# One of the two gate products of each attention tile moved between the turn of its probabilities and their products with the values

## The chip, the cores and the metric

The kernel runs on one core of a Trainium2 chip. The metric is the device time of one execution in microseconds (us). TensorE is called PE here, VectorE DVE, ScalarE ACT, GpSimd POOL and SyncE SP, as in the profile.

## The reference

Two blocks run one after the other over 256 tokens of width 1024, in fp32. The first has a convolution, a gated linear attention and a mixture of 64 experts. The second, in which the change lies, has a linear recurrence beside an attention over 64 selected keys, a feed-forward part and a last gate. Of the second block this matters:

```python
logits = logits + bias                                  # 8 heads, masked to the selected keys
probs = softmax(logits, axis=-1)
o = einsum('btngk,btknd->btngd', probs, v_sel)
yb = o @ w_attn_br
merged = sigmoid(gate_a) * ya + sigmoid(gate_b) * yb    # gate_b: 1024 columns of xn @ w_in
x = x + merged @ w_out
xn = rmsnorm(x, ffn_norm)
up = xn @ w_up
...
```

## The kernel before

Each engine has its program written out by hand, in one fixed order, and waits on named semaphores. The tokens form two tiles of 128 (t = 0 and 1).

**Tasks and banks.** Everything that PE computes is a task with a name, and a task takes one of the eight PSUM banks. The list `_tasks()` names all tasks in PE's order, and `_bank_table()` deals the banks out in turn: with eight banks, a task has the bank of the task eight places ahead of it in the list. `take_bank(task)` makes PE wait until that earlier task's bank was read out, `full(ins, task)` reports a result, and `wait_full` and `read` are the reader's side.

**The attention of the second block.** PE computes the logits, `log0_0` to `log0_3` for tile 0 and `log1_0` to `log1_3` for tile 1 (L1016), then two branch products `ya2`, `ya3`. DVE adds the bias to a bank of logits (L2085) and copies it out with the mask (L2088); that frees the bank. After the last one DVE takes the row maxima (L2091, L2093), ACT the exponentials (L1419), and DVE the inverse of the sums (L2097) and the scaling of the probabilities (L2099), which sets `probs_ready`. PE turns the probabilities by transposes, tasks `pt` (L1028), ACT copies them out (L1433), PE multiplies them with the values, tasks `pv` (L1035), and ACT copies these out (L1437). Tile 0 has 2 `pt` tasks, tile 1 has 4; each tile has 2 `pv` tasks. The gate products `gd0` to `gd3` (sigmoid of them is gate_b, L1092 on ACT) depend on none of this; PE does two of them behind each tile's `pv`.

ACT's order around it, which the change leaves alone, is this:

```python
for t in range(TT):
    ...                                   # 8 exponentials of tile t, L1419
    if t == 0: weights_high(1, "gd1")
    else: per_chunk(["gd0", "gd1"], ...)
    ...                                   # pt copies L1433, then pv copies L1437
    if t == 0: weights_high(1, "gd3")
```

**Weights in two parts.** A large weight is multiplied as a high and a low part. SP loads it into a ring (one unit of 2 MB), ACT rounds it to the high part in two halves (`weights_high`, L1107), and POOL subtracts to get the low part, in four pieces a half (`weights_low`, L533). A product task of this kind (L595) of 128x256 runs, for each of its two columns blocks, 16 matmuls with the high part and then 8 with the low part, 48 in all; the first wait for `high_ready`, the others for `low_ready`. Units are named after the last task that uses them: `gd1` serves gd0 and gd1, `gd3` serves gd2 and gd3, `yb1` and `yb3` the attention's output product (tasks `yb0` to `yb3`), `mo0_1` and `mo1_1` the merged output product (tasks `mo`). ACT makes the high part of `yb1` behind the rounding of both tiles' `pv` results (L1444, whose low part is L1584 on DVE), then that of `yb3`, `mo0_1` and `mo1_1`. POOL follows unit by unit; of `mo1_1` it does half and DVE the other half (L1584). After the `yb` tasks DVE gates them (L2117, L2120), ACT rounds (L1454), and PE goes on with `mo`, the turn L662, and the feed-forward products, all on L595.

The functions that the change touches follow.

Of the kernel before, what the change touches and what calls it, by code (L numbers as in the profile page):

```python
# [47 lines left out]
NH, NKV, HD = 8, 2, 128  # L48
# [26 lines left out]
def _tasks():  # L75
    names = []
    names += ["g0", "g1", "a0", "a1", "g2", "g3", "a2", "a3", "k0", "k1", "fl", "z0", "z1"]
    names += [f"v{u}_{t}" for u in range(2) for t in range(2)] + ["q0", "q1"]
    names += ["r0", "r1", "kdt0", "kdt1", "r2", "r3"] + [f"kv{i}" for i in range(8)] + ["ga0", "ga1"]
    names += [f"o{h}" for h in range(4)] + ["ga2", "ga3", "osum0", "osum1", "csum"]  # L80
    names += ["gb0", "gb1", "csq", "gb2", "gb3"]
    names += [f"yg{j}" for j in range(4)] + [f"yc{j}" for j in range(4)]
    names += [f"mix{u}_{t}" for t in range(2) for u in range(2)]
    names += ["x1t0", "x1t1", "lg0", "x1t2", "x1t3", "lg1", "pos"]
    first = list(names)
    n2 = [f"x2t{j}" for j in range(4)] + ["relb", "kiwi_k", "kiwi_w"]
    n2 += [f"lx{j}" for j in range(4)] + ["wi"] + [f"lg_{j}" for j in range(4)]
    n2 += ["kk", "vv", "qi0", "qi1"] + [f"dots{t}_{j}" for t in range(2) for j in range(4)]
    n2 += [f"lr{j}" for j in range(4)] + [f"li{j}" for j in range(4)]
    n2 += ["ksum"] + [f"qq{j}" for j in range(4)]  # L90
    n2 += ["gc0", "gc1"] + ["qsum"] + ["gc2", "gc3", "ya0", "ya1"]
    for t in range(2):
        n2 += [f"log{t}_{j}" for j in range(4)]
    n2 += ["ya2", "ya3"]
    for t in range(2):
        n2 += [f"pt{t}_{s}_{k}" for s in range(t + 1) for k in range(2)] + [f"pv{t}_{k}" for k in range(2)]
        n2 += [f"gd{2 * t}", f"gd{2 * t + 1}"]
    n2 += [f"yb{j}" for j in range(4)] + ["mo0_0", "mo1_0", "mo0_1", "x3t0", "x3t1", "mo1_1", "x3t2", "x3t3"]
    for i in range(6):
        n2 += [f"fg{i}_0", f"fg{i}_1", f"fu{i}_0", f"fu{i}_1"]  # L100
    n2 += [f"dn{u}_{t}" for u in range(2) for t in range(2)]
    for t in range(2):
        n2 += [f"x4t{2 * t}", f"x4t{2 * t + 1}"] + [f"pp{u}_{t}" for u in range(2)]
    n2 += [f"pg{u}_{t}" for t in range(2) for u in range(2)]
    return first, n2
# [41 lines left out]
def build(nc, a, out):  # L147
    with ExitStack() as ctx:
# [80 lines left out]
        v2 = slab[:, 7, 512:1024].rearrange("p (t n) -> p t n", t=TT)  # L229
# [12 lines left out]
        prob_t = slab[:, 5, :].rearrange("p (s h t) -> p s h t", s=TT, h=NH)  # L242
# [39 lines left out]
        def take_bank(task):  # L282

            b, use = BANK[task]
            if use:
                nc.tensor.wait_ge(S(f"bank_read{b}"), use)
            return bank(task)

        def full(ins, task):

            ins.then_inc(S(f"bank_full{BANK[task][0]}"), 1)
# [10 lines left out]
        def wait_read(eng, *tasks):  # L302

            for task in tasks:
                b, use = BANK[task]
                eng.wait_ge(S(f"bank_read{b}"), use + 1)
# [264 lines left out]
        def _(pe):  # L571
            mm = nc.tensor.matmul
            units = [0, 0]

            def unit(part=0, cols_=512):


                name = UNITS[part][units[part]]
                s = units[part] % STREAM
                units[part] += 1  # L580
                w = ring[:, s, :].rearrange("p (c n) -> p c n", n=cols_)
                if name not in SPLIT[part]:
                    wait_landed(pe, part, name)
                    return w
                high = ring[:, STREAM + SPLIT[part].index(name) % 2, :].rearrange("p (c n) -> p c n", n=cols_)
                return high, w, split_count(part, name)
# [29 lines left out]
                    ins = one(r32(low[:, c, wcol]), r32(x[0][:, c, xcol]), False, c == DC - 1)  # L616
                return ins

            def chan_major(w, x, tasks, arrive=None):

                for i, task in enumerate(tasks):
                    o = take_bank(task)
                    for m in range(2):
                        f = P * (2 * i + m)
                        last = products(o[:, T * m:T * m + T], w, x, False, slice(f, f + P), slice(0, T), i,
                                        arrive=None if i + m else arrive)
                    full(last, task)
# [40 lines left out]
            w = ring[:, 0, :].rearrange("p (c n) -> p c n", c=DC)  # L668
            chan_major(w, xT, ["g0"])
            w = unit()[:, :, 256:512]  # L670
# [10 lines left out]
            o = take_bank("fl")  # L681
            for c in range(DC):
                last = mm(o[0:RANK, 0:T], w_flr[:, c, :], xT[:, c, :], start=c == 0, stop=c == DC - 1)
# [3 lines left out]
            for j in range(2):  # L687
                o = take_bank(f"z{j}")
                for m in range(2):
                    f = P * (2 * j + m)  # L690
                    last = mm(o[:, T * m:T * m + T], slab[0:RANK, 10, f:f + P], slab[0:RANK, 10, 512:512 + T],
                              start=True, stop=True)
# [8 lines left out]
            for t in range(TT):  # L701
                o = take_bank(f"kdt{t}")
                for h in range(H1):
                    last = nc.tensor.transpose(o[:, P * h:P * h + P], half(5, 0)[:, h, P * t:P * t + P], ident[:])
# [4 lines left out]
            for n in range(NCH):  # L709
                b = CHUNK * (n % 2)  # L710
                for hp in range(2):
                    task = f"kv{2 * n + hp}"
                    o = take_bank(task)
                    for m in range(2):
                        h = 2 * hp + m
# [8 lines left out]
            for h in range(H1):  # L724
                o = take_bank(f"o{h}")
                for m in range(2):
                    for n in range(NCH):
                        st = states(n, h)[:, P * m:P * m + P]
                        last = mm(o[:, T * m + CHUNK * n:T * m + CHUNK * n + CHUNK], st,  # L729
                                  half(7, 0)[:, h, CHUNK * n:CHUNK * n + CHUNK], start=True, stop=True)  # L730
# [207 lines left out]
            xn = xn_parts  # L938
# [82 lines left out]
            for t in range(TT):  # L1021

                pe.wait_ge(S("probs_ready"), t + 1)
                for s in range(t + 1):
                    for k in range(2):
                        o = take_bank(f"pt{t}_{s}_{k}")
                        for m in range(4):
                            last = nc.tensor.transpose(o[:, P * m:P * m + P], lgt[:, 4 * k + m, P * s:P * s + P],  # L1028
                                                       ident[:])
                        full(last, f"pt{t}_{s}_{k}")  # L1030
                wait_read(pe, *[f"pt{t}_{s}_{k}" for s in range(t + 1) for k in range(2)])
                for k in range(2):
                    o = take_bank(f"pv{t}_{k}")
                    for s in range(t + 1):
                        last = mm(o[:, 0:512], v2[:, s, HD * k:HD * k + HD],  # L1035
                                  prob_t[:, s, 4 * k:4 * k + 4, :].rearrange("p h t -> p (h t)"),
                                  start=s == 0, stop=s == t)
                    full(last, f"pv{t}_{k}")
                chan_major(unit(1), xn, [f"gd{2 * t}", f"gd{2 * t + 1}"])
            pe.wait_ge(S("att_low"), 2)  # L1040
            chan_major(unit(1), att_parts, ["yb0", "yb1"])
            chan_major(unit(1), att_parts, ["yb2", "yb3"])
# [1254 lines left out]
```

## Time and profile before

| | |
|---|---|
| median of 3 runs | 1736.12 us (1735.61 to 1736.6) |
| time of the profiled execution | 1736.04 us |
| its span, first to last instruction | 1734.3 us |
| mean granted clock of PE | 0.89 |
| PE busy | 1363.6 us (79% of the span) |
| POOL busy | 609.2 us (35%) |
| ACT busy | 429.1 us (25%) |
| DVE busy | 423.0 us (24%) |

The time is 1.7 us above the span of the same execution. The shares are means over very different stages: the expert stage in the middle of the span waits for transfers, and the attention lies near 1,385 to 1,440 us, behind it. What the change is worth is read from that part and from what follows it. PE and PEld are the matmuls and the weight loads of the one TensorE; PEclk 1.00 is 2.4 GHz and 0.50 is 1.2 GHz.

### The profile page before, as it was taken

To read this page: it belongs to the slowest core of one execution; us is meant where nothing else is said; L and a number is where in the kernel's file an instruction comes from. 1 tells how busy PE (TensorE), PEld (TensorE's weight loads), DVE (VectorE), ACT (ScalarE), POOL (GpSimd) and SP (SyncE) were. 2 spreads that over 40 slices of the span, in tenths; PEclk is the share of its full clock that TensorE was granted. 3 is DMA by queue.
4 is the path that set the end of the run, shared out by engine and by line. 5 is a ranking of instruction groups with operands and counts; after the bars stand their busy time and mean duration, and the time that the engine had idled before them with its cause. 6 is when DMAs were issued, how large, how long until landed. Compare 5 with 4: busy or idle time off the path is not lost.

```text
span 1734.3 us, 21607 instructions
## 1 busy us (share of the span) xinstructions
PE 1363.6 (79%) x9196; PEld 983.1 (57%) x9196; DVE 423.0 (24%) x901; ACT 429.1 (25%) x542; POOL 609.2 (35%) x485
## 2 busy tenths in 40 slices
PE   7999998677557746675666576657799999899998
PEld 7899996333123313331333133222699988899986
DVE  3995554000000000000000000000416642233203
ACT  4444741000000000000000000000547563544434
POOL 6886790000000000000000000000587958688894
PEclk9999999888788878877888788778899999999999
DMA  9453477999999999999999999999445444455551
GB/s 366 147 192 108 176 270 293 384 428 428 427 429 428 428 429 428 429 429 429 429 428 428 429 428 429 429 428 419 164 167 209 156 161 146 146 195 187 176 192 54
DMA packets 46058, 539.56 MB, mean 311 GB/s; under 512 B 4440, under 2 KB 8544, under 8 KB 14624
## 3 DMA queue, kind: packets, MB, share of 16 engines
q1 hardware_dynamic: 42704, 532.44, 75.5%
q0 software_dynamic: 1184, 3.94, 0.6%
q10 hardware_dynamic: 2096, 2.11, 0.4%
q8 instruction: 56, 0.92, 0.2%
q14 instruction: 18, 0.15, 0.0%
HBM read 537.41 MB, written 1.06 MB: 310 GB/s over the span
## 4 chain that ended last, share of the span: by engine, by line
PE 64%; DMA 30%; DVE 2%; SPq 1%; ACT 1%; issue 1%; POOL 1%; DVEq 0%; ACTq 0%
PE bank L595 38%; DMA ring<-in_w 18%; PE bank L823 13%; DMA slab<-in_w 10%; PE bank L808 6%; PE bank L880 2%; DMA ring<-in_units 1%; SPq L408 1%; PE bank L869 1%; POOL ring_parts L533 1%; ACT ring_parts L1107 0%; PE bank L1035 0%; PE bank L989 0%; PE bank L729 0%; PE bank L835 0%
## 5 line engine op out<-in xcount | busy, mean ns | idle before, releaser
L533 POOL TENSOR_TENSOR ring_parts<-ring,ring_parts 128x512 fp32r<-128x512 f32 x448 | 594.6, 1366 | 1007.2 <-ACT ring_parts L1107 1007.1
L595 PE MATMUL bank<-slab_parts,ring_parts 128*128 128x256 f32 x3328 | 498.2, 285 | 2.1 <-DVE rows_parts L1968 2.1
L595 PEld LDWEIGHTS bank<-slab_parts,ring_parts 128*128 128x128 f32 x3328 | 458.1, 193 | 4.4 <-issue 3.1
L823 PE MATMUL bank<-ring,slab 128*32 128x512 f32 x1472 | 254.9, 674 | 168.6 <-DMA slab<-in_w 88.1
L823 PEld LDWEIGHTS bank<-ring,slab 128*32 128x32 f32 x1472 | 68.4, 122 | 340.8 <-issue 339.1
L1107 ACT ACTIVATE ring_parts<-ring 128x2048 fp32r<-128x2048 f32 x114 | 212.0, 1910 | 169.5 <-PE bank L595 167.2
L869 PE MATMUL bank<-ring,slab 128*32 128x512 f32 x752 | 139.2, 724 | 140.5 <-DMA slab<-in_w 70.5
L595 PE MATMUL bank<-rows_parts,ring_parts 128*128 128x256 f32 x752 | 187.2, 286 | 0.0
L869 PEld LDWEIGHTS bank<-ring,slab 128*32 128x32 f32 x752 | 37.4, 130 | 226.1 <-issue 225.4
L595 PE MATMUL bank<-ring_parts,slab_parts 128*128 128x512 f32 (+1 forms) x672 | 160.5, 388 | 3.9 <-POOL ring_parts L533 2.8
L1868 DVE TENSOR_TENSOR slab<-slab,bank 128x512 f32<-128x512 f32 x16 | 11.0, 687 | 578.7 <-PE bank L823 578.7
L595 PEld LDWEIGHTS bank<-rows_parts,ring_parts 128*128 128x128 f32 x752 | 146.5, 195 | 0.5 <-issue 0.5
L595 PEld LDWEIGHTS bank<-ring_parts,slab_parts 128*128 128x128 f32 x672 | 125.7, 190 | 31.7 <-POOL ring_parts L533 3.7
L823 PE MATMUL bank<-slab 128*32 128x512 f32 x512 | 130.5, 668 | 0.0
L808 PEld LDWEIGHTS bank<-slab 128*128 128x128 f32 x512 | 124.2, 334 | 7.4 <-issue 4.2
L808 PE MATMUL bank<-slab 128*128 128x128 f32 x512 | 122.9, 401 | 1.5 <-DVE slab L1851 1.5
L1546 DVE SCALAR_TENSOR_TENSOR bank<-slab,cols,bank 128x255 f32<-128x255 f32 (+28 forms) x232 | 88.0, 468 | 0.1
L1224 ACT ACTIVATE slab<-bank 128x512 f32<-128x512 f32 x16 | 9.6, 597 | 282.6 <-PE bank L823 276.6
L1232 ACT ACTIVATE slab<-bank 128x512 f32<-128x512 f32 x16 | 9.6, 597 | 282.0 <-PE bank L869 282.0
L1876 DVE COPY slab<-bank 128x512 f32<-128x512 f32 x16 | 11.1, 692 | 276.3 <-PE bank L869 276.3
L869 PE MATMUL bank<-slab 128*32 128x512 f32 x272 | 74.6, 709 | 4.0 <-DMA slab<-in_w 3.4
L1220 ACT ACTIVATE slab<-bank 128x512 f32<-128x512 f32 x16 | 9.6, 597 | 272.0 <-PE bank L823 260.2
(302 smaller groups left out, 941.5 us busy)
## 6 DMA issues: line engine op xcount, KB each, us to landing
ring<-in_w SPq DMA_DIRECT2D x143, 2048.0 KB, 19.8
ring<-in_units SPq DMA_DIRECT2D x59, 2048.0 KB, 8.4
slab<-in_w SPq DMA_DIRECT2D x49, 2048.0 KB, 25.3
ring<-in_units SPq DMA_DIRECT2D x2, 1024.0 KB, 9.2
slab<-bias_scratch ACTq DMA_DIRECT2D x2, 1024.0 KB, 8.6
slab<-in_xT SPq DMA_DIRECT2D x1, 1024.0 KB, 5.0
rows<-in_ln_g POOLq DMA_DIRECT2D x2, 512.0 KB, 17.9
slab<-in_x SPq DMA_DIRECT2D x1, 1024.0 KB, 5.3
```

Source lines behind the costliest of these rows:

```text
L408: sp.dma_start(dst, src).then_inc(S(f"expert_landed{step % 2}{j}" if place is None else "apart_landed"), 16)
L533: ins = g.tensor_tensor(r32(w_q), w_q, r32(high_q), ALU.subtract)
L595: return mm(out_, l, r, start=start and first, stop=stop and last)
L808: last = mm(b[:, P * (c % 4):P * (c % 4) + P], tok(0)[:, t, c::DC], sel[:, t, :, :].rearrange("p j s -> p (j s)"), start=t == 0, stop=t == 1)
L823: last = mm(b[CAP * j:CAP * j + CAP, :], xg[:, c, CAP * j:CAP * j + CAP], wt[j][:, c, :], start=c == 0, stop=c == DC - 1, tile_position=(0 ...
L869: last = mm(b[CAP * j:CAP * j + CAP, :], hid_t[:, m, CAP * j:CAP * j + CAP], wt[j][:, 512 * hf:512 * hf + 512], start=m == 0, stop=m == 3, ...
L880: last = mm(acc[t][hf][:], spread[:, P * t:P * t + P], y_sb[:, 512 * hf:512 * hf + 512], start=False, stop=ends, skip_group_check=again)
L1107: A(r32(high), w, ACT.Copy).then_inc(S("high_ready"), 1)
L1220: A(slab[:, 1, 0:512], low_bank[:], ACT.Copy).then_inc(S("xg0_copied"), 1)
L1546: ins = stt(out_, src[:, c, 0:T - lag], wc, sum_[:, lag:T], ALU.mult, ALU.add)
L1868: tt(hid, silu_sb, up_bank[:], ALU.mult).then_inc(S("hid_ready"), 1)
L1876: v.tensor_copy(y_sb[:, 512:1024], high_bank[:]).then_inc(S("y1_copied"), 1)
```

## The change

The task list, and with it the banks, and the order on PE. The second gate product of a tile stays where it was; the first goes ahead of the tile's `pv` tasks. Nothing is computed differently, and no instruction is added or dropped.

```diff
     for t in range(2):
-        n2 += [f"pt{t}_{s}_{k}" for s in range(t + 1) for k in range(2)] + [f"pv{t}_{k}" for k in range(2)]
-        n2 += [f"gd{2 * t}", f"gd{2 * t + 1}"]
+        n2 += [f"pt{t}_{s}_{k}" for s in range(t + 1) for k in range(2)]
+        n2 += [f"gd{2 * t}"] + [f"pv{t}_{k}" for k in range(2)] + [f"gd{2 * t + 1}"]
...
-            def chan_major(w, x, tasks, arrive=None):
+            def chan_major(w, x, tasks, arrive=None, between=None):
 
                 for i, task in enumerate(tasks):
+                    if i and between:
+                        between()
                     o = take_bank(task)
...
-                wait_read(pe, *[f"pt{t}_{s}_{k}" for s in range(t + 1) for k in range(2)])
-                for k in range(2):
-                    o = take_bank(f"pv{t}_{k}")
-                    for s in range(t + 1):
-                        last = mm(o[:, 0:512], v2[:, s, HD * k:HD * k + HD],
-                                  prob_t[:, s, 4 * k:4 * k + 4, :].rearrange("p h t -> p (h t)"),
-                                  start=s == 0, stop=s == t)
-                    full(last, f"pv{t}_{k}")
-                chan_major(unit(1), xn, [f"gd{2 * t}", f"gd{2 * t + 1}"])
+                def values(t=t):
+                    wait_read(pe, *[f"pt{t}_{s}_{k}" for s in range(t + 1) for k in range(2)])
+                    for k in range(2):
+                        o = take_bank(f"pv{t}_{k}")
+                        for s in range(t + 1):
+                            last = mm(o[:, 0:512], v2[:, s, HD * k:HD * k + HD],
+                                      prob_t[:, s, 4 * k:4 * k + 4, :].rearrange("p h t -> p (h t)"),
+                                      start=s == 0, stop=s == t)
+                        full(last, f"pv{t}_{k}")
+                chan_major(unit(1), xn, [f"gd{2 * t}", f"gd{2 * t + 1}"], between=values)
```

On PE, at tile 0, the order before is as follows: L1028 is `pt`, L1035 is `pv`, L595 here is `gd0`. `bank_readN` is the wait for bank N to be read out. The banks of the logits are visible in the list: `log1_0` has bank 4, `log1_1` bank 5, `log1_2` bank 0, `log1_3` bank 1.

```order
L1028 MATMUL bank2<-ident,slab 128x128 [waits bank_read2,probs_ready]
L1028 MATMUL bank2<-ident,slab 128x128 x3
L1028 MATMUL bank3<-ident,slab 128x128 [waits bank_read3]
L1028 MATMUL bank3<-ident,slab 128x128 x3
L1035 MATMUL bank4<-slab 128x512 [waits bank_read4,bank_read3,bank_read2]
L1035 MATMUL bank5<-slab 128x512 [waits bank_read5]
L595 MATMUL bank0<-slab_parts,ring_parts 128x256 [waits high_ready,bank_read0]
```

The same place now (L1030 is `pt`, L1038 is `pv`, L595 with bank 4 is `gd0` and with bank 1 is `gd1`; the other matmuls of `gd0`, alike, are left out):

```order
L1030 MATMUL bank2<-ident,slab 128x128 [waits bank_read2,probs_ready]
L1030 MATMUL bank2<-ident,slab 128x128 x3
L1030 MATMUL bank3<-ident,slab 128x128 [waits bank_read3]
L1030 MATMUL bank3<-ident,slab 128x128 x3
L595 MATMUL bank4<-slab_parts,ring_parts 128x256 [waits high_ready,bank_read4]
...
L1038 MATMUL bank5<-slab 128x512 [waits bank_read5,bank_read3,bank_read2]
L1038 MATMUL bank0<-slab 128x512 [waits bank_read0]
L595 MATMUL bank1<-slab_parts,ring_parts 128x256 [waits high_ready,bank_read1]
```

`gd0` stands where the first `pv` task stood, and has its bank, 4; the two `pv` tasks have banks 5 and 0. `gd2` and the `pv` tasks of tile 1 change in the same way.

On ACT the order is the same before and after; this is its piece from tile 0's last exponentials to tile 1's first (L1107 makes high parts, first those of `gd1`, then those of `gd3`; L1433 copies `pt`, L1437 `pv`), before:

```order
L1107 ACTIVATE ring_parts<-ring 128x8x256 [waits bank_full1,unit_landed1]
L1107 ACTIVATE ring_parts<-ring 128x8x256
L1433 ACTIVATE slab<-bank2 128x512 [waits bank_full2]
L1433 ACTIVATE slab<-bank3 128x512 [waits bank_full3]
L1437 ACTIVATE slab<-bank4 128x4x128 [waits bank_full4]
L1437 ACTIVATE slab<-bank5 128x4x128 [waits bank_full5]
L1107 ACTIVATE ring_parts<-ring 128x8x256 [waits bank_full7,unit_landed2]
L1107 ACTIVATE ring_parts<-ring 128x8x256
L1419 ACTIVATE slab,small<-slab,small 128x256 [waits rowmax_ready]
L1419 ACTIVATE slab,small<-slab,small 128x256 x7
```

Only the banks that the two `pv` copies wait for are others now (5 and 0).

## Rows read from the trace of the kernel before

**Rows 1.** The page: busy shares, and PE, clock in 40 slices
```profile
PE 1363.6 (79%) x9196; PEld 983.1 (57%) x9196; DVE 423.0 (24%) x901; ACT 429.1 (25%) x542; POOL 609.2 (35%) x485
PE   7999998677557746675666576657799999899998
PEclk9999999888788878877888788778899999999999
```

**Rows 2.** Chain that ended last, merged, 1380 to 1735: start, length, what
```profile
1401.66 0.89 PE bank L1028 x8
...
1403.69 0.70 DVE slab L2088
...
1404.53 3.50 PE bank L1035 x4
1408.02 11.71 PE bank L595 x96
...
1422.63 3.67 PE bank L1035 x8
1426.30 34.56 PE bank L595 x288
...
1464.86 7.08 POOL ring_parts L533 x4
...
1492.00 206.02 PE bank L595 x1440
```

**Rows 3.** PE in order of time: start, length, ..., [idle before it <-releaser]
```profile
1404.53 3.50 PE L1035 MATMUL bank<-slab 128*128 128x512 f32 x4 [1.99 <-DVE slab L2088]
...
1419.56 1.91 PE L1028 MATMUL bank<-ident,slab 128*128 128x128 f32 x16
1422.63 3.67 PE L1035 MATMUL bank<-slab 128*128 128x512 f32 x8 [1.16 <-ACT slab L1433]
```

**Rows 4.** DVE in order of time, 1403 to 1419
```profile
1403.69 0.69 DVE L2088 TENSOR_TENSOR slab<-bank,slab 128x512 f32<-128x512 f32 x1
1405.21 0.69 DVE L2088 TENSOR_TENSOR slab<-bank,slab 128x512 f32<-128x512 f32 x1
1411.38 0.47 DVE L2093 TENSOR_SCALAR small<-small 128x8 f32<-128x8 f32 x1
1416.46 2.54 DVE L2099 TENSOR_TENSOR slab<-slab,small 128x2048 f32<-128x2048 f32 x1
```

**Rows 5.** ACT in order of time, 1406 to 1429
```profile
1408.06 0.60 ACT L1437 ACTIVATE slab<-bank 128x512 f32<-128x512 f32 x1 [1.25 <-PE bank L1035]
1408.56 3.71 ACT L1107 ACTIVATE ring_parts<-ring 128x2048 fp32r<-128x2048 f32 x2
1412.16 0.49 ACT L1419 ACTIVATE slab<-slab,small 128x256 f32<-128x256 f32 x1
...
1426.34 0.60 ACT L1437 ACTIVATE slab<-bank 128x512 f32<-128x512 f32 x1 [1.12 <-PE bank L1035]
1427.05 2.01 ACT L1444 ACTIVATE slab_parts<-slab 128x1024 fp32r<-128x1024 f32 x2
1428.97 3.70 ACT L1107 ACTIVATE ring_parts<-ring 128x2048 fp32r<-128x2048 f32 x2
```

**Rows 6.** Windows: sum, PE, PEld, DVE, ACT, POOL busy (count), PEclk, DMA share, GB/s
```profile
1401.50:1404.93 3.43, 1.44 (x11) 1.09 (x10) 2.13 (x5) 1.09 (x2) 3.43 (x4) 1.00 0.69 177
1404.93:1408.35 3.42, 3.42 (x7) 1.32 (x6) 3.32 (x8) 0.89 (x2) 2.98 (x3) 0.50 0.96 412
1485.90:1492.00 6.10, 1.27 (x8) 0.86 (x9) 2.23 (x8) 4.98 (x14) 4.03 (x4) 0.86 0.92 325
1492.00:1497.10 5.10, 5.10 (x24) 5.10 (x25) 0.78 (x4) 4.95 (x3) 3.67 (x3) 0.50 0.13 51
```

**Rows 7.** POOL in order of time, 1430 to 1472
```profile
1430.94 20.11 POOL L533 TENSOR_TENSOR ring_parts<-ring,ring_parts 128x512 fp32r<-128x512 f32 x16 [8.33 <-ACT ring_parts L1107]
1451.44 10.95 POOL L533 TENSOR_TENSOR ring_parts<-ring,ring_parts 128x512 fp32r<-128x512 f32 x8 [0.40 <-ACT ring_parts L1107]
1464.86 7.07 POOL L533 TENSOR_TENSOR ring_parts<-ring,ring_parts 128x512 fp32r<-128x512 f32 x4 [2.46 <-ACT ring_parts L1107]
```

**Rows 8.** Waits of PE, 1400 to 1493: who <- whom, total us, times, longest
```profile
PE bank L662 <- ACT slab L1288: 2.8, 1, 2.8
PE bank L595 <- DVE rows_parts L1968: 2.1, 1, 2.1
PE bank L595 <- POOL ring_parts L533: 1.4, 1, 1.4
```

**Rows 9.** DVE in order of time, beside POOL's last four pieces
```profile
1466.62 2.93 DVE L1584 TENSOR_TENSOR ring_parts<-ring,ring_parts 128x2048 fp32r<-128x2048 f32 x1 [2.91 <-ACT ring_parts L1107]
```

## The prediction

> **What bounds the kernel now.** I read the page first: PE is busy for 79% of the span, and in the last ten slices for nine tenths or more nearly throughout, so there the time is PE's own work and its short waits [rows 1]. Then the chain that ended last. From the turn of tile 0's probabilities to the end it goes through PE almost everywhere, and from 1492.00 it is 206.02 us of feed-forward products without a break [rows 2]. So what is late at 1492 is late at the end by as much, and the question is by how much the change moves that point.
>
> Next, PE in order of time, for the idle time that the change is to fill. There are two places. Behind tile 0's transposes PE idles 1.99 us, released by DVE's L2088; behind tile 1's it idles 1.16 us, released by ACT's copy L1433 [rows 3]. They are not alike. In the first, PE waits for the bank of log1_0, which L2088 reads out until 1404.38; ACT's two copies are long done. The second bank follows at 1405.90 [rows 4].
>
> Then DVE and ACT, for what tile 1's transposes wait for. ACT copies pv0_1 from 1408.06, makes the high part of gd3 from 1408.56 and starts tile 1's exponentials at 1412.16, directly behind it [rows 5]. The row maxima were there at 1411.85, 0.3 us ahead. DVE then has the probabilities ready at 1416.46 + 2.54 = 1419.00 [rows 4], and PE comes to them at 1419.56 [rows 3]. ACT's queue is thus within 0.6 us of being the bound, and the copy of pv0_1 is an early link of it.
>
> **First gap: not filled.** By the order shown above, gd0 takes bank 4, the bank of log1_0. So gd0 waits for the same L2088 as pv0_0 did and starts at 1404.53 too. The 1.99 us stay.
>
> **Tile 0 behind the gap.** A matmul of a product task takes 0.12 us at full clock: 288 of them in 34.56 us [rows 2]. gd0 has 48, so 5.76 us. But the granted clock fell to 0.50 at 1404.93, after a stretch in which PE was busy for 1.44 of 3.43 us, and stayed there until 1408.35, with PE busy all through it [rows 6]. That stretch ahead is the same now, so the fall comes too and costs half of 3.42 us, 1.7 us. (If it doesn't, this is 0.) gd0 ends at 1404.53 + 5.76 + 1.7 = 1412.0. The eight pv matmul records of tile 1 took 3.67 us with a tail of some 0.2, so 0.43 each [rows 3]; the four of tile 0 take 1.7 us at full clock. They end at 1413.7, or 1413.85 with the tail. Before, they ended at 1408.02 [rows 2]. The copies of pv0 on ACT are 5.8 us late.
>
> **What is queued behind that copy.** On ACT: gd3's high part and tile 1's exponentials; nothing there has slack any more. Behind them DVE's two steps. So probs_ready moves from 1419.00 to 1424.8. PE itself is done with gd1 at 1413.7 + 5.76 = 1419.5 and then stands idle for 5.4 us. It had run from 1404.53 to 1419.56 before, and runs to 1419.5 now: what it won by not waiting for the banks of log1_1 and log1_2 between the pv tasks, it lost in gd0 under the low clock.
>
> **Tile 1.** PE turns from 1424.9 (before: 1419.56): 5.3 us late. The second gap, of 1.16 us, is filled by gd2, that is a true gain (its bank is that of gd0, which ACT reads behind the exponentials, by about 1424). But the clock has fallen by then. After 6.10 us with 1.27 us of work, PE ran 5.10 us at 0.50 [rows 6], which costs 2.55 us; after the shorter gap it cost 1.7. This gap of 5.4 us was never seen here; between the two I take 2.1. Turn 1.77 (16 transposes, their row less its tail), gd2 5.76, clock 2.1, pv1 3.4: pv1 ends at 1437.95, with its tail 1438.1. Before it ended at 1426.30 [rows 2]. That is 11.8 us late, of which 5.76 are gd2 moved ahead of it. PE ends gd3 at 1437.95 + 5.76 = 1443.7. Before it was 1426.14 + 96 x 0.12 = 1437.7. PE is 6.0 us late.
>
> **Weights.** ACT rounds the attention's result and makes yb1's high part only behind the last pv copy: L1444 at 1427.05, L1107 at 1428.97 [rows 5]; POOL starts on it at 1430.94, after 8.33 us idle [rows 7]. The first half of yb1's low part is there four pieces later, 1430.94 + 20.11 / 4 = 1435.97. All this moves by 11.8, to 1447.8. PE wants it at 1443.7 + 16 x 0.12 = 1445.6. Before, it had slack of 3.7 us; now PE waits 2.2, and is 8.2 us late from there.
>
> POOL is late by 11.8 us in yb1 and yb3. Its idle times behind that, 0.40 and 2.46 us [rows 7], absorb 2.9: it ends mo1_1's half 8.95 us late. There PE waited for POOL for 1.4 us already [rows 8], so PE's own 8.2 would count as 6.8. POOL's 8.95 counts.
>
> **The sum.** Copies of pv0 5.8 late; less 0.5 of slack at the turn, 5.3. From the turn's start to pv1's end 13.2 (1.8 + 5.8 + 2.1 + 3.4 and the tail) instead of 6.7 (1419.56 to 1426.30), so 6.5 more: 11.8. Less 2.9 of POOL's idle time: +8.95. The profiled execution had 1736.04, so 1745.0; that execution lies 0.1 below the median of the runs. SP, DVE's and POOL's queues keep their orders. SP's loads hang on gd1 (same time), gd3 and yb1 (6 to 9 us late), and these units are used tens of us later; they cost nothing.
>
> **A price weighed.** POOL's last four pieces took 7.07 us and the sixteen ahead 20.11, so 1.77 against 1.26 each [rows 7]. The last ran beside DVE's half of mo1_1, 2.93 us from 1466.62 [rows 9]. The Trainium skill (SBUF — State Buffer, "Who interferes with whom") says that a DVE instruction with two inputs in SBUF contends with a GpSimd instruction that reads SBUF; by it the overlap decides the price. If DVE's half fell outside POOL's, these pieces would take 5.03 and the sum be 6.9, so 1742.9. Both hang on ACT's one queue as before, so I keep 7.07.
>
> **Rivals.** *The same mechanism at full clock.* Neither fall of the clock costs: -1.7 - 2.1, so +5.1, 1741.2. For it: waits of 1.16 and 1.4 us had no such cost. Against it: 1.99 us had. With only one fall or a cheaper POOL it is 1742.5 to 1743.5. Chance 0.3 for this group, 0.48 for the forecast with both.
>
> *More falls.* PE now idles 1.4 + 2.2 = 3.6 us ahead of mo1_0's low part. If the clock falls there too, 1.7 more: 1746.7, and another behind yb0's wait 1748. Chance 0.1.
>
> *The gaps are filled and the softmax isn't late* (faster). If ACT could do gd3's high part and the exponentials ahead of pv0's copies, or gd0 started at 1402.54, PE would run without a break: from 1404.53, gd0 to gd3, pv0, pt1, pv1 are 23.04 + 1.7 + 1.8 + 3.4 = 29.9, end 1434.5 instead of 1437.7. POOL's idle time of 2.46 limits what this gives to 2.5 us: 1733.5. It decides when pv0's copies end by about 1408.7. Against it: ACT's program puts the copies first, and PE's puts gd0 ahead of them. Chance 0.04. [...]
>
> *Absorbed.* POOL and ACT give more back than their idle times say, and less than 3.5 us is left: 1736 to 1739.5. For it: POOL waited 8.33 us ahead of yb1's low part, so its queue is not full. Against it: the feed-forward part is solid PE. Chance 0.08. That the change does nothing is out: PE's order and the banks are others.
>
> **The numbers.** A measurement here tells about 0.2%, 3.5 us, from no change. Likeliest 1745.0. The range 1739.8 to 1748.3 leaves out the faster and most of the absorbed case, and the double fall. Its own range for the slow group is 1741 to 1747. Faster 0.04, same 0.08, slower 0.88.
>
> **What would show it.** Right: PE's first L595 behind tile 0's transposes still waits 2.0 us for DVE's L2088; ACT's pv0 copy near 1413.8; tile 1's exponentials near 1418; PE idle for some 5 us ahead of tile 1's transposes, released by DVE's L2099; no wait ahead of pv1; a new wait for POOL near 1446; the long feed-forward stretch starts near 1501. Wrong: the exponentials of tile 1 still near 1412, no idle time ahead of the turn, or POOL's low part of yb1 on time.

## The result and the profile after

The changed kernel took 1749.15 us (median of 4 runs, 1746.67 to 1754.2), the kernel before 1736.17 (4 runs, 1735.61 to 1736.6). The ratio is 1.007, with a 95% interval of 1.005 to 1.009. The change makes the kernel slower, by 13 us. 1745.0 had been forecast, in a range up to 1748.3.

The profiled execution took 1754.2 us, more than the median, and 4.5 us of that arose ahead of the changed part, which starts at 1405.96 instead of 1401.50. In the router stage, from 279.5 to 289.7 us, its PE ran at a granted clock of 0.50, the one of before at 0.95. The programs are alike up to the second block, and in all 17 profiles taken the two go together: the clock in this window is 0.50 to 0.67 in the six whose changed part starts at 1405.96 or later, and 0.94 or more in the eleven that reach it by 1403.90. So I don't put this delay down to the change. The times of the kernel before fall into groups as well (of 22 runs beside the first experiments, 15 lie from 1735.15 to 1738.19, 6 from 1740.4 to 1741.09, one at 1745.53), but no slower one was profiled, so that this is the same delay is likely and not shown. I therefore read all traces by one stretch that lies behind it, from the first transpose of tile 0 to the first matmul of the long feed-forward part, and call it **the stretch**. It starts, on PE in order of time, in the kernel before at

```profile
1401.50 1.04 PE L1028 MATMUL bank<-ident,slab 128*128 128x128 f32 x8
```

and ends at 1492.00 [rows 2], so 90.50 us. In the changed kernel PE in order of time shows this (L1030 is the turn, L1038 the values, L664 the later turn; the bracket is the idle time ahead and who ended it):

```profile
1405.96 1.04 PE L1030 MATMUL bank<-ident,slab 128*128 128x128 f32 x8
1408.89 0.38 PE L595 MATMUL bank<-slab_parts,ring_parts 128*128 128x256 f32 x1 [1.90 <-DVE slab L2091]
...
1429.08 3.67 PE L1030 MATMUL bank<-ident,slab 128*128 128x128 f32 x16 [5.21 <-DVE slab L2102]
...
1451.92 21.37 PE L595 MATMUL bank<-slab_parts,ring_parts 128*128 128x256 f32 x176 [2.03 <-POOL ring_parts L533]
1477.49 11.36 PE L595 MATMUL bank<-ring_parts,slab_parts 128*128 128x512 f32 x40 [4.19 <-issue]
1490.33 7.55 PE L595 MATMUL bank<-ring_parts,slab_parts 128*128 128x512 f32 x32 [1.47 <-POOL ring_parts L533]
1507.03 1.27 PE L664 MATMUL bank<-ident,slab 128*128 128x128 f32 x8 [2.81 <-ACT slab L1291]
1510.36 0.55 PE L595 MATMUL bank<-slab_parts,ring_parts 128*128 128x256 f32 x1 [2.05 <-DVE rows_parts L1971]
```

The stretch is 1510.36 - 1405.96 = 104.40 us: 13.90 more. Of the two old gaps the first is still there (1.90, released by DVE, as 1.99 was in [rows 3]); the second is gone. Three new ones stand beside them: 5.21 us ahead of tile 1's turn, 2.03 for POOL's low part of yb1, both as forecast, and 4.19 us ahead of `mo0_0`, which was not. Its "issue" says only that the profile saw no releaser.

ACT and DVE in order of time, in the changed kernel:

```profile
1418.16 0.60 ACT L1440 ACTIVATE slab<-bank 128x512 f32<-128x512 f32 x1 [0.26 <-PE bank L1038]
1418.65 3.71 ACT L1110 ACTIVATE ring_parts<-ring 128x2048 fp32r<-128x2048 f32 x2
1422.26 0.49 ACT L1422 ACTIVATE slab<-slab,small 128x256 f32<-128x256 f32 x1
...
1442.26 0.60 ACT L1440 ACTIVATE slab<-bank 128x512 f32<-128x512 f32 x1 [1.12 <-PE bank L1038]
```

Counted from the start of the stretch, pv0's last copy comes at 12.20 (before 6.56), tile 1's exponentials at 16.30 (before 10.66), pv1's last copy at 36.30 (before 24.84). The chain of steps forecast is there: the copy, gd3's high part, the exponentials, one behind the other.

DVE:

```profile
1426.55 2.47 DVE L2102 TENSOR_TENSOR slab<-slab,small 128x2048 f32<-128x2048 f32 x1
...
1466.17 11.22 DVE L1587 TENSOR_TENSOR slab_parts<-slab,slab_parts 128x512 fp32r<-128x512 f32 x1 [2.93 <-ACT slab_parts L1457]
1477.31 0.69 DVE L2120 TENSOR_TENSOR bank<-bank,slab 128x512 f32<-128x512 f32 x1
...
1478.64 0.68 DVE L1587 TENSOR_TENSOR slab_parts<-slab,slab_parts 128x512 fp32r<-128x512 f32 x1
```

The second of these rows is the surprise. It is one subtraction of 128x512, the low part of the first quarter of the merged result. The same instruction for the next quarter took 0.68 us, 12 us later (the last of these rows), and in the kernel before it was this:

```profile
1453.72 0.83 DVE L1584 TENSOR_TENSOR slab_parts<-slab,slab_parts 128x512 fp32r<-128x512 f32 x1 [2.92 <-ACT slab_parts L1454]
```

Now it stands for 11.22, and DVE's gating of `yb2` and `yb3` (L2120) and everything behind it stand behind it. POOL at the same time:

```profile
1446.87 29.98 POOL L533 TENSOR_TENSOR ring_parts<-ring,ring_parts 128x512 fp32r<-128x512 f32 x24 [14.26 <-ACT ring_parts L1110]
1483.20 7.07 POOL L533 TENSOR_TENSOR ring_parts<-ring,ring_parts 128x512 fp32r<-128x512 f32 x4 [6.36 <-ACT ring_parts L1110]
```

In [rows 7] POOL did 16 pieces, paused for 0.40 us and did 8 more. Now 24 run in one, at 1.25 us each, and DVE's instruction ends 0.5 us after POOL's last. I call this **the lockout**: DVE asks for SBUF while POOL's pieces follow each other without a break, and gets in when they stop. That became the theory to test, against two others: that lateness alone costs 13.9 us, or that DVE's instruction was long by itself.

### The profile page after: what moved, and what is told of

Its sections match the earlier page's. It is cut to its first block, busy times and chain, and to the rows that moved or that the text cites. A ratio compares the mean times of both kernels' runs of the same rounds, so it can differ in the third digit from the quotient of the medians.

```text
span 1752.5 us, 21607 instructions
## 1 busy us (share of the span) xinstructions
PE 1374.7 (78%) x9196; PEld 991.4 (57%) x9196; DVE 432.3 (25%) x901; ACT 429.3 (24%) x542; POOL 608.5 (35%) x485
## 4 chain that ended last, share of the span: by engine, by line
PE 64%; DMA 29%; DVE 2%; ACT 2%; issue 2%; SPq 1%; POOL 1%; DVEq 0%; ACTq 0%
PE bank L595 36%; DMA ring<-in_w 15%; DMA slab<-in_w 13%; PE bank L825 13%; PE bank L810 6%; PE bank L882 3%; SPq L408 1%; POOL ring_parts L533 1%; ACT ring_parts L1110 1%; PE bank L871 1%; DMA ring<-in_units 0%; PE bank L991 0%; PE bank L731 0%; PE bank L837 0%; PE bank L790 0%
## 5 line engine op out<-in xcount | busy, mean ns | idle before, releaser
L595 PE MATMUL bank<-slab_parts,ring_parts 128*128 128x256 f32 x3328 | 500.8, 285 | 6.0 <-DVE rows_parts L1971 2.1
L595 PEld LDWEIGHTS bank<-slab_parts,ring_parts 128*128 128x128 f32 x3328 | 459.7, 193 | 8.0 <-issue 3.3
L595 PE MATMUL bank<-rows_parts,ring_parts 128*128 128x256 f32 x752 | 188.5, 287 | 0.0
L595 PE MATMUL bank<-ring_parts,slab_parts 128*128 128x512 f32 (+1 forms) x672 | 162.2, 391 | 7.8 <-issue 4.4
L595 PEld LDWEIGHTS bank<-rows_parts,ring_parts 128*128 128x128 f32 x752 | 147.6, 196 | 0.7 <-issue 0.7
L595 PEld LDWEIGHTS bank<-ring_parts,slab_parts 128*128 128x128 f32 x672 | 126.4, 191 | 36.8 <-issue 5.7
L1879 DVE COPY slab<-bank 128x512 f32<-128x512 f32 x16 | 11.1, 691 | 278.9 <-PE bank L871 278.9
## 6 DMA issues: line engine op xcount, KB each, us to landing
rows<-in_ln_g POOLq DMA_DIRECT2D x2, 512.0 KB, 17.9
```

Of the source, the lines that this page charges most:

```text
L595: return mm(out_, l, r, start=start and first, stop=stop and last)
L1879: v.tensor_copy(y_sb[:, 512:1024], high_bank[:]).then_inc(S("y1_copied"), 1)
```

## The experiments

All were timed beside the kernel before. The difference in the stretch is against 90.50.

### The changed kernel again

> The changed kernel itself, once more, since its four runs spread over 7.5 us (1746.7 to 1754.2) and those of before over 1.0. Theory A (late weights plus a lockout): POOL's 24 low-part pieces of yb1, yb3 and mo0_1 run without a break, and DVE's first low part of the merged result stands for some 11 us until they end; this comes every time, the runs lie near 1749.5, and the profile shows one instruction of L1587 of over 5 us. Theory B (late weights alone, the lockout is chance): some runs, and perhaps this profile, lack the long instruction and lie at 1744 to 1746. Upstream, the profiled execution of the result lost 4 us in the router stage to a fall of the clock; that should be absent from most runs.

1754.69 us (6 runs, 1750.53 to 1756.04), ratio 1.0089 (1.0068 to 1.0109). The stretch is 1406.91 to 1511.38, 104.47: +13.97. L1587 stands for 11.23 us. The stretch is the same to 0.1 us in both profiles, so what these two differ by is upstream of it. That is not all that spreads. The lowest of the first four runs, 1746.67, lies 3.3 us below 1736.04 + 13.90, which a delay upstream can't explain. It wasn't profiled; two later profiles show what can be absent in single executions, a fall of the clock and the long instruction itself.

### Each tile alone

```diff
-        n2 += [f"gd{2 * t}"] + [f"pv{t}_{k}" for k in range(2)] + [f"gd{2 * t + 1}"]
+        pv = [f"pv{t}_{k}" for k in range(2)]
+        n2 += [f"gd{2 * t}"] + pv + [f"gd{2 * t + 1}"] if t == 0 else pv + [f"gd{2 * t}", f"gd{2 * t + 1}"]
...
+                if t != 0:
+                    values()
-                chan_major(unit(1), xn, [f"gd{2 * t}", f"gd{2 * t + 1}"], between=values)
+                chan_major(unit(1), xn, [f"gd{2 * t}", f"gd{2 * t + 1}"], between=values if t == 0 else None)
```

(with 1 in place of 0 for the other tile).

> Only tile 0 has its first gate product ahead of the pv tasks; tile 1 keeps pv1 first. Both theories: pv0's copies 5.8 us late, exponentials and the turn of tile 1 late by 5.3, the clock at half for the turn and pv1, so pv1's end some 7.3 late, and yb1's weights with it; PE still has slack there (3.7). Theory A: POOL and PE are late by about the same, the 0.4 us pause of POOL ahead of mo0_1's pieces stays, so there is no lockout: 5.9 more, 1742. Theory that any lateness of POOL brings the lockout: 1747 or more, with a long L1587.

> Only tile 1 has its first gate product ahead of the pv tasks. Both theories: the 1.16 us gap is filled, pv1's end 4.4 us late, yb1's low part 4.4 late, PE waits 2.0 for it. Late weights alone: POOL's idle times absorb 2.9, +1.5: 1737.7. Theory A: POOL's work on yb1, yb3 and mo0_1 now runs without a break (the 0.4 us pause is gone) and DVE's first low part of the merged result is locked out until it ends, some 11 us; that puts the last one 7 us late: 1743. The profile shows a long L1587 or not.

Tile 0 alone: 1743.5 us (12 runs from 1742.0), 1.0041 (1.0025 to 1.0057); the stretch +6.6, where 5.9 was reckoned. PE waits 5.21 us ahead of the turn. POOL keeps its pause of 0.40 us, and no low part of 128x512 (L1590 in this file) is over 1.1 us.

Tile 1 alone: 1744.35 us (10 runs from 1742.92), 1.0039 (1.0024 to 1.0054); the stretch +6.9, where lateness alone was to cost 1.5 and with the lockout 7. POOL's 24 pieces are in one run (29.98 us), and L1590 stands for 11.21 us. The half of the change that does what it is written for, filling the second gap, costs as much as the other.

### ACT's order

The copies of `pv` become a function, and tile 0's are called behind tile 1's exponentials:

```diff
+                    take_values(0)
                     wait_full(act, "ya3")
...
-                for k in range(2):
-                    o = wait_full(act, f"pv{t}_{k}")
...
+                def take_values(t):
+                    for k in range(2):
+                        o = wait_full(act, f"pv{t}_{k}")
...
                 if t == 0:
                     weights_high(1, "gd3")
+                else:
+                    take_values(1)
```

> The changed kernel, with ACT's program in another order: gd3's high part and tile 1's exponentials come ahead of the copies of pv0. Both theories: the exponentials start at their row maxima again (7 us after L2088's first bank, as before), PE's idle time of 5.2 us ahead of tile 1's turn is gone, and with it the second fall of the clock; pv1's end is then late by 4.3 only. Late weights alone: 1737.6. Theory A: POOL runs 24 pieces without a break all the same, long L1587: 1743. If the exponentials weren't held by the pv0 copies: as the changed kernel, 1749.

1748.47 us (7 runs, 1743.1 to 1755.53), 1.007 (1.0045 to 1.0094); the stretch +7.4. The exponentials start 10.3 us into it (1417.11 against 1406.81), before 10.66, changed 16.30, and PE waits 0.76 instead of 5.21 ahead of the turn. So it was ACT's queue. The 0.76 us that are left are a small case of the same thing: POOL's pieces of gd1 and gd3 now follow each other in one run, and DVE's scaling of the probabilities, 2.54 us in [rows 4], takes 4.00:

```profile
1403.31 19.97 POOL L533 TENSOR_TENSOR ring_parts<-ring,ring_parts 128x512 fp32r<-128x512 f32 x16 [9.88 <-ACT ring_parts L1110]
```

```profile
1416.70 0.38 DVE L2100 TENSOR_SCALAR small<-small 128x8 f32<-128x8 f32 x1
...
1421.43 4.00 DVE L2106 TENSOR_TENSOR slab<-slab,small 128x2048 f32<-128x2048 f32 x1
```

The run of 24 is there, and a low part of 9.71 us with it. The medians of this kernel and of the changed one can't be told apart, since the upstream delay lies over them; the stretch can, 97.9 against 104.4.

### A pause for POOL, and lateness without the change

```diff
-            weights_low(1, *SPLIT[1][SPLIT[1].index("gd1"):])
+            weights_low(1, "gd1", "gd3", "yb1", "yb3")
+            pool.wait_ge(S("merged2_low"), 1)
+            weights_low(1, *SPLIT[1][SPLIT[1].index("mo0_1"):])
```

> The changed kernel with one more wait on POOL: ahead of mo0_1's pieces it waits until DVE has made the first low part of the merged result. DVE asks for it at about the time when POOL ends yb3. Theory A (lockout by POOL's unbroken run): the long L1587 is gone (under 2 us), POOL loses 0.7 us, the merged result is ready some 6 us earlier, mo1_1 bounds: 5.6 less than the changed kernel, that is 8 to 9 above before, 1744 to 1745 in the runs without the upstream delay. If the lockout is something else: mo0_1's pieces start later for nothing, 1749 to 1750.

1746.61 us (6 runs from 1745.03), 1.0059 (1.004 to 1.0078). DVE and POOL in order of time:

```profile
1462.44 1.28 DVE L1589 TENSOR_TENSOR slab_parts<-slab,slab_parts 128x512 fp32r<-128x512 f32 x1 [2.92 <-ACT slab_parts L1459]
1465.19 1.72 DVE L1589 TENSOR_TENSOR slab_parts<-slab,slab_parts 128x512 fp32r<-128x512 f32 x1
```

```profile
1443.13 20.05 POOL L533 TENSOR_TENSOR ring_parts<-ring,ring_parts 128x512 fp32r<-128x512 f32 x16 [14.23 <-ACT ring_parts L1112]
1463.80 18.43 POOL L533 TENSOR_TENSOR ring_parts<-ring,ring_parts 128x512 fp32r<-128x512 f32 x12 [0.63 <-DVE slab_parts L1589]
```

One pause of 0.63 us, and the instruction of 11.22 us takes 1.28. The stretch is +9.57, 4.3 less than in the changed kernel. Less its own pause it is +8.9, close to the sum of the forecast.

The other way round, the kernel before with POOL held up until PE has ended gd3 (tasks, banks and order on all other engines untouched):

```diff
-            weights_low(1, *SPLIT[1][SPLIT[1].index("gd1"):])
+            weights_low(1, "gd1", "gd3")
+            wait_full(pool, "gd3")
+            weights_low(1, *SPLIT[1][SPLIT[1].index("yb1"):])
```

> The kernel before, with one wait more on POOL: it starts yb1's pieces only when PE has ended gd3 (1437.8 instead of 1430.9), and nothing else moves. PE then waits 3.3 us for yb1's low part. Late weights alone: POOL 6.9 late, less 2.9 of its idle time, +4.0: 1740.1. Theory A: POOL's 24 pieces run without a break, DVE's low part is locked out until 1468, the last gated product of yb3 comes 9.5 us late: 1745.5, with a L1584 of about 11 us in the profile.

1746.28 us (6 runs from 1745.12), 1.0055 (1.0037 to 1.0072); the stretch +9.51, the forecast +9.5.

```profile
1458.30 9.93 DVE L1586 TENSOR_TENSOR slab_parts<-slab,slab_parts 128x512 fp32r<-128x512 f32 x1 [2.92 <-ACT slab_parts L1456]
```

```profile
1437.74 29.94 POOL L533 TENSOR_TENSOR ring_parts<-ring,ring_parts 128x512 fp32r<-128x512 f32 x24 [15.25 <-PE bank L597]
```

So the lockout belongs to POOL's run, not to the gate products.

### The first gap, and the clock behind the second

```diff
-        b = turn_.pop(0)
-        turn_.append(b)
+        if name == "gd0":
+            b = table["pt0_0_0"][0]
+        else:
+            b = turn_.pop(0)
+            turn_.append(b)
```

> The changed kernel, but gd0 has the bank of pt0_0_0 instead of that of log1_0, so it waits for ACT's first copy (at about 0.2 us behind the transposes) and no longer for DVE's L2088. Expected: the 1.9 us gap nearly gone, and with it the first fall of the clock (1.7); pv0's copies, the exponentials and all behind them 3.4 to 3.6 us earlier than in the changed kernel; the idle time ahead of tile 1's turn stays 5.2, since both its ends move; the lockout stays. 3.5 below the changed kernel: 1745.7. If the gap were worth nothing: 1749.2.

1749.13 us (6 runs from 1746.42), 1.0063 (1.0045 to 1.0081); the stretch 101.16, 3.2 below the changed kernel. PE in order of time:

```profile
1407.63 0.38 PE L598 MATMUL bank<-slab_parts,ring_parts 128*128 128x256 f32 x1 [0.25 <-ACT slab L1439]
1426.33 3.67 PE L1033 MATMUL bank<-ident,slab 128*128 128x128 f32 x16 [5.21 <-DVE slab L2105]
```

The first gap was the bank's, as read from the order. Filling it takes 1.65 us off the gap, and the first fall of the clock goes with it: gd0 starts 5.85 us ahead of pv0, where it was 7.35. The second gap only moves, and is 5.21 as before.

```diff
-                    for m in range(2):
+                    for m in [0, 1] * (2 if task == "gd1" else 1):
```

> The changed kernel, but PE computes gd1 twice into the same bank (48 matmuls more, 5.76 us, the result the same), which fills its idle time of 5.2 us ahead of tile 1's turn with work. If the second fall of the clock comes from that idle time, it is gone: the turn starts 0.5 us later, and pv1 ends 1.3 to 1.6 us earlier than in the changed kernel; with the lockout bound behind POOL's start, the whole is 1.3 to 1.6 below it. If the fall has another cause, 0.5 above it.

1750.79 us (6 runs, 1742.42 to 1753.89), 1.0078 (1.006 to 1.0097). The profiled execution is the one of 1742.42, and it shows something else than it was made for:

```profile
1460.29 1.00 DVE L1587 TENSOR_TENSOR slab_parts<-slab,slab_parts 128x512 fp32r<-128x512 f32 x1 [2.92 <-ACT slab_parts L1457]
```

```profile
1439.48 31.38 POOL L533 TENSOR_TENSOR ring_parts<-ring,ring_parts 128x512 fp32r<-128x512 f32 x24 [12.47 <-ACT ring_parts L1110]
```

Here DVE got in within a run of 24 pieces, which took 1.4 us more than elsewhere. So an unbroken run makes the lockout likely, not certain. The stretch is +6.4. Neither fall of the clock is in this trace; the second would be missing by the added work, the first is missing by itself (the gap of 1.90 us is there). For what the second fall alone costs, this run is inconclusive.

### Many pauses, and the repairs together

```diff
                         ins.then_inc(S("low_ready"), 1)
+                        if part == 1:
+                            wait_low(pool, split_count(part, name) + h + 1)
```

> The changed kernel; in the second block POOL waits, after each half's four pieces, for its own last piece before it issues the next. If the lockout comes of POOL's pieces following each other without a break, DVE gets in at the next half's end at the latest: no L1587 over 5 us, POOL some 0.1 us slower in each half, 4 to 5 us less than the changed kernel: 1745 to 1746 in the runs without the upstream delay. If DVE's chance does not depend on breaks: L1587 of 8 to 11 us, 1750.

> The control for it: the kernel before with the same waits of POOL. No lockout there to remove. POOL is on the path only with mo1_1's half, so at most 0.1 to 0.4 us for each pause that lies there: 1736 to 1737.

The changed kernel with it: 1746.67 us (6 runs from 1745.57), 1.0062 (1.0042 to 1.0083); the longest single low part of 128x512 takes 1.71 us; the stretch +8.95. That is not all the waits' doing: the first fall of the clock is absent in this execution, though the gap of 1.90 us is there, and the turn comes 1.3 us earlier for it.

```profile
1461.51 1.66 DVE L1589 TENSOR_TENSOR slab_parts<-slab,slab_parts 128x512 fp32r<-128x512 f32 x1 [2.93 <-ACT slab_parts L1459]
1464.42 1.71 DVE L1589 TENSOR_TENSOR slab_parts<-slab,slab_parts 128x512 fp32r<-128x512 f32 x1
```

The control, the kernel before with the same waits: 1740.82 us (12 runs, in two groups like those of the kernel before beside it, whose median is 1738.76), 1.0002 (0.999 to 1.0015), the stretch +0.2. No cost of the waits can be told from the times, and the lockout is gone.

> The kernel before, with POOL starting yb1's pieces only when PE has ended gd3, and with POOL's wait after each half's four pieces. With before_pool_late it had 9.5 us more between tile 0's turn and the feed-forward part, 4.0 of them reckoned as lateness and the rest as lockout. If that split is right, the lockout goes and 4.0 to 4.6 stay: 1740.5. If lateness alone costs what it cost there: 1745.5.

> Only tile 1's first gate product ahead of its pv tasks, with POOL's wait after each half. 6.9 us were lost without that wait. If lateness is 1.5 of it and lockout the rest: 1.5 to 2.3 above before, 1738. If not: 1743.

These two are the kernels of POOL's late start and of tile 1 alone, with the same waits. Late start: 1742.82 us (11 runs), 1.0033 (1.0019 to 1.0046); the stretch +5.95 instead of +9.51. Tile 1: 1739.93 us (12 runs), 1.0013 (1.0002 to 1.0025); +2.8 instead of +6.9. So 3.6 and 4.1 us go with the lockout. What stays lies 1.35 and 0.5 us above the upper ends of what was reckoned for lateness (4.6 and 2.3). In the first, PE's clock fell behind its wait of 3.26 us, and once more at the last turn (1.97 us for 8 transposes, 1.27 in the kernel before), which the reckoning left out; for the second I found no one place.

> The changed kernel with all three repairs: ACT's other order, the early bank for gd0, and POOL's wait after each half. The exponentials are on time, PE turns tile 1 some 0.8 us earlier than before, pv1 ends 3.5 late since gd2 is ahead of it, no lockout: 1 to 2 above before, 1737 to 1738. If the lockout stays: 1742 to 1743.

> The change at tile 0 alone, with ACT's other order and the early bank for gd0. The first gap is filled, the clock's first fall gone, the exponentials on time; PE then waits for them some 2 to 3 us ahead of the turn, which starts 0.5 to 0.9 us earlier than before. POOL keeps its pause, no lockout. 0.5 to 0.9 below before if that wait costs no clock, 1735.5; 1 us above if it does.

All repairs with both tiles: 1742.23 us (12 runs from 1738.48), 1.0027 (1.0014 to 1.0041), the stretch +2.8, a miss too: 1 to 2 had been expected, with the turn 0.8 us earlier than before, and it is 0.2 earlier. The tile-0 version without the waits: 1742.2 us, 1.0024 (1.0012 to 1.0037), the stretch +8.6, a miss. PE waited 8.45 us ahead of the turn, and DVE and POOL show why:

```profile
1416.17 6.64 DVE L2106 TENSOR_SCALAR small<-small 128x8 f32<-128x8 f32 x1
```

```profile
1402.79 20.00 POOL L537 TENSOR_TENSOR ring_parts<-ring,ring_parts 128x512 fp32r<-128x512 f32 x16 [9.80 <-ACT ring_parts L1116]
```

An operation on 8 numbers a partition, 0.47 us in [rows 4], stands for 6.64 and ends as POOL's run ends, at 1422.8. Making gd3's high part early had joined POOL's pieces of gd1 and gd3 into one run. With ACT's order alone there was the same run of 16, and the same scaling, asked for 13.4 us into it as here, took 0.38 us (the row of L2100 above). So the lockout can strike or not at the same place of an equal run.

> The change at tile 0 alone with ACT's other order, the early bank and POOL's wait after each half. Without that wait, a scaling of the row maxima (L2106, 128 by 8) stood for 6.6 us until POOL's run of 16 pieces on gd1 and gd3 had ended. If that too is the lockout, it now takes under 5 us, mostly under 1.5; the turn of tile 1 comes 17 to 17.5 us behind tile 0's (18.06 before), and the time is 0 to 1 us below before: 1735 to 1736 in the runs without the upstream delay. If it is something else: 1741 or more.

With the waits it takes 0.66 us:

```profile
1413.43 0.66 DVE L2108 TENSOR_SCALAR small<-small 128x8 f32<-128x8 f32 x1
```

1740.01 us (12 runs from 1735.69), 1.0007 (0.9995 to 1.0019); the stretch +1.3, where -1 to 0 was expected. The turn comes 17.84 us into it (18.06 before), but the clock is down to half there, behind a wait of 3.07 us, and the turn takes 3.61 us where it took 1.91 [rows 3]. No version was found that beats the kernel before.

## Why the prediction was wrong

**Right.** The first gap stays, since gd0 has the bank of log1_0: 1.90 us, and it goes when the bank does. Of the steps reckoned, each counted from the start of the stretch:

| step | forecast | measured |
|---|---|---|
| pv0's copies late | 5.8 | 5.6 |
| tile 1's turn late | 5.3 | 5.1 |
| PE idle ahead of the turn | 5.4 | 5.2 |
| pv1's end late | 11.8 | 11.5 |
| PE's wait for yb1's low part | 2.2 | 2.0 |
| POOL's half of mo1_1 late | 8.95 | 13.9 |

The clock behaved as [rows 6] had shown. The windows of the changed kernel (PE, PEld, DVE, ACT and POOL busy, clock, DMA):

```profile
1405.90:1409.30 3.40, 1.50 (x13) 1.26 (x13) 2.04 (x5) 1.09 (x2) 3.40 (x4) 1.00 0.65 173
1409.30:1412.70 3.40, 3.40 (x18) 3.40 (x18) 3.30 (x8) 0.00 (x0) 3.14 (x3) 0.51 0.99 424
1423.90:1429.10 5.20, 0.02 (x1) 0.02 (x1) 2.68 (x2) 4.87 (x15) 5.20 (x4) 0.75 0.83 277
1429.10:1433.20 4.10, 4.10 (x20) 4.10 (x21) 0.00 (x0) 2.20 (x4) 3.51 (x3) 0.50 0.37 160
```

It is at half behind the gap of 1.90 us, with PE busy all through, and again behind the one of 5.21, through tile 1's turn: 3.67 us for 16 transposes where it had been 1.91 [rows 3]. The direction was right, and so was the mechanism up to POOL's start on yb1.

**Wrong.** The step that failed is this: "Its idle times behind that, 0.40 and 2.46 us [rows 7], absorb 2.9: it ends mo1_1's half 8.95 us late." I took POOL's pause of 0.40 us for slack to be used up. Without it DVE's first low part of the merged result waited for eight of POOL's pieces, yb2's and yb3's gating came behind it, mo1_1's high part with them, and POOL idled 6.36 us ahead of its last pieces instead of 2.46. So POOL's idle times absorbed nothing: 11.5 us late at its start, it was 13.9 late at its end.

With a pause put back ahead of mo0_1's pieces the same stretch is +9.57. So 4.3 us of the 13.9 are the lockout, or 5.0 with that pause of 0.63 us counted out, and 8.9 to 9.6 are lateness, where 8.95 was forecast. That the lower of these meets the forecast is in part luck: in that trace POOL starts on yb1 11.4 us late instead of 11.8, and its 28 pieces take 0.35 us more than in [rows 7]. The +8.95 with the waits behind each half is no second proof of the sum, since a fall of the clock was missing there and POOL started 0.9 us earlier.

How the pause helps is not that DVE uses its 0.40 us. In the kernel before DVE asks 2.3 us behind it, at 1453.72, while POOL's run of eight is on, and gets in. In the stretch, in the traces where POOL does not wait for its own pieces, every subtraction and scaling of DVE with its operands in SBUF that was asked for up to 11.5 us into a run of POOL got in within about a piece. The ones that waited until the run ended were all asked for 13.4 us or more into it, nine in number; of those asked for so late only the ones of 0.38 and 1.00 us above got in, and DVE's next ones in the latter's run. What the pause does, by this, is to begin a new run shortly before DVE asks. That is read from where the cases lie; the place in the run was not varied by itself.

The prediction did weigh that DVE and POOL contend, but only as what DVE takes from POOL (1.77 us a piece against 1.26). What POOL can take from DVE it left at the durations of [rows 9] and their like. The Trainium skill (SBUF — State Buffer, "SBUF: two separate sides") says that the shared pair of ports is held for a whole instruction while the other engine fully blocks. Read so, a DVE instruction waits for one piece, by these traces at most 1.3 us (an estimate). The traces differ from that, and they decide: DVE waited over some eight in a row, in 6 of the 7 profiles with POOL's run of 24 pieces and no waits between them. No run here shows that it is the ports that DVE waits for.

**The rivals.** That the gaps are filled and the softmax isn't late is refuted by the idle times above. Absorption is, too. More falls of the clock did come (0.54 from 1477.4 to 1480.8, behind the 4.19 us), but PE still waited 1.47 us for POOL there, so they cost nothing.

**Left open.** What decides whether DVE gets in late in a run: it did in one of the seven profiles, and a scaling did in one of two alike. And the cause of the upstream delay of some 4.5 us.

## What to carry to other kernels

A short idle time of an engine can be what another engine lives on: ahead of moving work into it, or of letting an upstream delay eat it, ask who else reads and writes SBUF meanwhile. An independent product put ahead of a dependent one delays everything that stands behind the reader of the dependent one, here ACT's copy, the exponentials and the next weights, and that reader's queue sets the price, not PE's gap. A filled gap also needs a free bank, and the bank follows from the place in the list.

## What the runs showed of the hardware

Subtractions on POOL in one unbroken run of 16 to 24 pieces of 1.25 us could keep a DVE instruction with operands in SBUF waiting until the run ended; the recorded length was 6.6 to 11.2 us in seven cases. It hit a subtraction of 128x512 (0.68 us otherwise) and a scaling of 128x8 (0.17 to 0.67 otherwise). It is not certain: the subtraction took 1.00 us in one of seven runs of 24, and the scaling 0.38 at the same place of another run of 16. All such waits began 13.4 us or more into POOL's run. A reduction over 128x2048 (2.29 us, 11.1 us into a run of 16) and a reciprocal of 128x8 (0.20 us, 17.9 us into it) took their usual time. DVE's gating instructions with an operand in PSUM, earlier in the same runs of POOL, took their usual 0.69 to 0.70 us. A wait of POOL for its own last piece, every four pieces, left no such case in the five versions of the change or of POOL's late start that got it (longest single subtraction of 128x512 1.72 us), and it lengthened the stretch of the kernel before by 0.2 us. A fall of PE's clock behind the same gap of 1.90 us was there in some profiles (gd0 takes 7.35 us until pv0) and absent in two (5.86). And the profiles with a granted clock of 0.50 to 0.67 from 279.5 to 289.7 us came 4.5 to 5.4 us later to the changed part than the kernel before.
